# Four PSUM banks for logits and two for transposes, in place of two and four, in the first attention stage

## What is computed

```
_, sel = lax.top_k(score, k_top)
kv_sel = jax.vmap(lambda ck, ix: ck[ix])(c_kv, sel)
logits = jnp.einsum('bqhr,bqkr->bhqk', qa, kv_sel).astype(jnp.float32)
logits = logits + jnp.moveaxis(bias, -1, 1)
logits = jnp.where(valid[:, None], logits, -jnp.inf)
p = jax.nn.softmax(logits, axis=-1).astype(kv_sel.dtype)
return jnp.einsum('bhqk,bqkr->bqhr', p, kv_sel)
```

## Time and profile before

| what | value |
| --- | --- |
| median of 3 runs | 4300.61 us (4289.83 to 4303.97) |
| profiled execution, its own time | 4292.6 us |
| span of that execution | 4290.8 us |
| PE matmul busy | 3502.0 us (82%) |
| DVE busy | 2117.6 us (49%) |
| ACT busy | 2040.5 us (48%) |
| granted clock of PE, mean over the span | 0.906 |
| first attention stage (a_att) | 1238 to 2156 us of the span |
| second attention stage (b_att) | 3195 to 3997 us of the span |

### The profile page before, as it was taken

The page is one execution under the profiler, slowest core; times in us unless marked ns, Lnnn a source line. Parts: engine busy times, 40 slices in busy tenths (PEclk is TensorE's granted clock), DMA queues, the critical chain, the costliest instruction groups (busy, mean ns, idle before and its releaser), DMA issues. The chain is left out here.

```text
span 4290.8 us, 64366 instructions
## 1 busy us (share of the span) xinstructions
PE 3502.0 (82%) x18498; PEld 2627.5 (61%) x18498; DVE 2117.6 (49%) x5809; ACT 2040.5 (48%) x3499; POOL 524.7 (12%) x560
## 2 busy tenths in 40 slices
PE   5598577764049999999969499999988888899699
PEld 5487455653036666666658478888975555555587
DVE  0401288999955555555556500000017777777344
ACT  0412267988447777777722401111126666666322
POOL 0011000551001111111101011111100000000011
PEclk9898898865569999999989799999999999999789
DMA  5222533872012222222245222222221111110343
GB/s 121 99 67 65 173 70 123 227 211 80 27 52 82 77 77 76 76 74 75 65 165 176 98 76 71 73 71 71 69 76 46 43 43 47 43 48 29 120 132 113
DMA packets 361723, 378.40 MB, mean 88 GB/s; under 512 B 71792, under 2 KB 291344, under 8 KB 359952
## 3 DMA queue, kind: packets, MB, share of 16 engines
q1 hardware_dynamic: 361488, 375.35, 29.5%
HBM read 237.89 MB, written 137.36 MB: 87 GB/s over the span
## 5 line engine op out<-in xcount | busy, mean ns | idle before, releaser
L1002 DVE CUSTOM_DVE_ANT_0 a_att_sb_lg<-a_att_ps_s,mask 128x512 f32<-128x512 f32 (+3 forms) x512 | 302.7, 595 | 283.3 <-PE a_att_ps_s L896 240.3
L895 PE MATMUL a_att_ps_s<-a_att_sb_k,a_att_sb_q 128*128 128x512 f32 (+3 forms) x640 | 291.3, 455 | 169.9 <-DMA a_att_sb_k<-scratch_kT 153.5
L1076 ACT ACTIVATE a_att_sb_pT<-a_att_ps_t 128x512 f32<-128x512 f32 (+3 forms) x640 | 317.0, 530 | 146.6 <-PE a_att_ps_t L912 138.7
L494 ACT ACTIVATE b_qkgv_sb_o_lo<-b_qkgv_ps_acc 128x512 f32<-128x512 f32 x128 | 76.6, 598 | 637.7 <-PE b_qkgv_ps_acc L477 472.6
L912 PE MATMUL a_att_ps_t<-ident,a_att_sb_lg 128*128 128x128 f32 x2176 | 345.5, 282 | 38.6 <-issue 29.4
L1068 ACT ACTIVATE b_att_sb_lg<-b_att_sb_lg,b_att_sb_negm 128x384 f32<-128x384 f32 (+15 forms) x256 | 305.7, 1199 | 110.9 <-DVE b_att_sb_negm L1010 110.1
L1004 DVE TENSOR_SCALAR_CACHE_REDUCE b_att_sb_lg<-b_att_ps_s 128x512 f32<-128x512 f32 (+3 forms) x512 | 289.7, 591 | 137.4 <-PE b_att_ps_s L901 131.4
L1033 DVE MEMSET b_att_sb_mx<- 128x256 f32 x1 | 0.3, 272 | 721.8 <-PEq L88 721.8
L1068 ACT ACTIVATE a_att_sb_lg<-a_att_sb_lg,a_att_sb_negm 128x384 f32<-128x384 f32 (+15 forms) x256 | 307.4, 1201 | 81.6 <-DVE a_att_sb_negm L1010 81.6
L912 PEld LDWEIGHTS a_att_ps_t<-ident,a_att_sb_lg 128*128 128x128 f32 x2176 | 252.0, 142 | 148.7 <-issue 100.4
L901 PE MATMUL b_att_ps_s<-b_att_sb_k,b_att_sb_q 64*128 64x512 f32 (+3 forms) x1280 | 323.2, 592 | 14.0 <-DMA b_att_sb_k<-scratch_kT 9.9
(11 more groups left out here) (273 smaller groups left out, 7135.1 us busy)
## 6 DMA issues: line engine op xcount, KB each, us to landing
select_sb_mod_w<-in_mod_w SPq DMA_DIRECT2D x16, 1024.0 KB, 7.1
a_att_sb_q<-scratch_qT SPq DMA_DIRECT2D x128, 128.0 KB
a_att_sb_q<-scratch_qT SPq DMA_DIRECT2D x256, 64.0 KB
a_att_sb_k<-scratch_kT SPq DMA_DIRECT2D x64, 256.0 KB
b_qkgv_sb_w<-in_b_w_in SPq DMA_DIRECT2D x32, 512.0 KB
mod_sb_w<-in_mod_w SPq DMA_DIRECT2D x4, 2048.0 KB, 8.7
scratch_gateT<-a_gate_sb_o_lo SPq DMA_DIRECT2D x32, 256.0 KB, 2.4
scratch_qT<-select_sb_o_hi SPq DMA_DIRECT2D x32, 256.0 KB, 3.4
```

The costliest lines, as they stand in the source:

```text
L895: nc.tensor.matmul(out, q[:, p // 2 % QS, 0, cols], k[:, slot, a:z], start=True, stop=False)
L1002: x = nc.vector.tensor_tensor_reduce(out, src, tab, 1.0, 2 * NEG, ALU.add, ALU.max, top[:, col:col + 1])
L1076: nc.scalar.activation(pT[:, r % 2, a:z, c:c + P], t_ps[:, n % TR, 0:z - a], ACT.Copy).then_inc(t_left, 1)
```

## The change

In `stage_attention`, the ring of logits in PSUM has four chunks and the ring of transposes two quads, for both callers. For `b_att` these were the numbers before, so only `a_att` changes.

```
     V2 = M == 1
     width = HD if V2 else P
-    SR, TR = (2, 4) if V2 else (4, 2)
+    SR, TR = 4, 2
     NCHUNK = M * BEFORE[NB]
```

## The result

| | before | changed |
| --- | --- | --- |
| median | 4298.69 us (20 runs, 4289.0 to 4309.37) | 4312.85 us (20 runs, 4303.7 to 4320.28) |
| ratio to before | | 1.0031, interval 1.0023 to 1.004 |
| span of the profiled execution | 4290.8 us | 4318.2 us |
| first attention stage in it | 918 us | 930.5 us |

What follows compares the result with a forecast made beforehand. PE was taken as the bound of `a_att`. 1.1 + 1.3 - 0.2 = 2.2 us a head, 35 us in 16 heads, gave 4328 on the profiled execution or 4336 on the median, written as 4332; range 4301 to 4370.

Steps and rivals of the forecast that it cites:

- What bounds the kernel: In `a_att`, PE bounds: head 7 busy 55.8 of 57 us; its stops wait for DVE or would wait for ACT's copies.
- the rival on the clock: Stops of 1 us cost PE its clock in two places of each head: 4 to 5 us a head more, 4400; chance 0.03.
- Part 1: Two more logits banks: all 48.8 us of PE's waits for DVE go; no wait for the fourth chunk back.
- Part 2, place 4: Two transpose banks fewer, head 7: T(3,0) starts at 51.02 instead of 51.01, so zero late; savings of earlier chunks are lost.
- Part 2, places 5 and 6: T(4,2) waits for the copy of T(4,0), 0.3 us late; the saved 0.9 us are gone.
- Part 2, places 7 to 9: Chain through maximum, exponential and copy: T(5,2) 0.6 us late, T(6,2) 1.3, T(7,2) 1.1.
- The ring stops: Places 10 to 13: four waits for a transpose bank, 1.3 us together, against two DVE waits of 0.1 us that go.
- The sum: All heads of `a_att`: 1.1 + 1.3 - 0.2 = 2.2 us a head, 35 us in 16 heads.
- heads of 59 to 60 us: Sign expected in the profile after the change: `a_att` heads take 59 to 60 us; 57 us or shorter would refute the forecast.
- the two cancel: Rival: gain and loss cancel within 0.3%, 13 us, at the lower bound or a little less; chance 0.10.
- The bound below: Places 5 to 9 hold PE up nowhere, 1.3 us ring stops stay, 0.9 us returns: +0.4 us a head, 6 us.
- ACT as the bound of the large places: Rival: ACT's copies are pulled apart and exponentials queue at places 5 to 9: +64 us, 4365; chance 0.12.

## Why the prediction was right in sign and wrong in size

- *What bounds the kernel* held: PE, and its two sorts of stop. DVE as the releaser is gone, ACT has come, in eight places of a head, the longest 1.1 us, as foretold; the 4.1 us a head are just above the 2.5 to 4. The mean clock of the stage stayed at 0.97 and that of head 7 at 1.00, so the rival on the clock can go.
- *Part 1* held: no wait for the fourth chunk back.
- *Part 2, place 4*: T(3,0) 0.05 us late, forecast zero, but by luck. The prediction read that T(3,0) before already ended on the copy of T(2,0). With four transpose banks it does not wait for that copy, and its row has no idle time in front; it came right behind S(5,0), which had waited 0.31 us for DVE. With two banks it does wait. ACT in the changed kernel:

```profile
1662.28 0.19 ACT L1068 ACTIVATION_READ_ACCUMULATOR a_att_sb_lg<-a_att_sb_lg,a_att_sb_negm  x1
1662.37 0.96 ACT L1076 ACTIVATE a_att_sb_pT<-a_att_ps_t 128x512 f32<-128x512 f32 x2
```

  The profile puts T(3,0)'s stop of 0.97 us down to the exponential, but that had ended 0.59 us before T(3,0) began (1663.06). The copy of T(2,0), about 0.6 us from 1662.37, had ended 0.09 before. The 0.05 us for a release, read from that coincidence, held all the same: T(5,2) began at 1674.00, the copy of T(5,0) at 1673.35, and such a copy takes 0.60. The stop at T(3,0) is there in nine heads, 8.7 us together, where the waits put down to the exponential rose by 8.4.
- *Part 2, places 5 and 6* is the step that failed. It said that the maximum of place 5 would get "only about 0.1 us earlier", because DVE has two chunks to do first, and that T(4,2) would be 0.3 late. DVE's timeline at place 5, before and then changed (the one piece of S(5,1) with the read of its maximum, the first piece of S(5,2), and after rows left out the maximum of the place):

```profile
1653.24 0.69 DVE L1002 CUSTOM_DVE_ANT_0 a_att_sb_lg<-a_att_ps_s,mask 128x512 f32<-128x512 f32 x1
1653.86 0.08 DVE L1002 DVE_READ_ACCUMULATOR2_ANT a_att_sb_mx<- 128x1 f32 x1
1654.30 0.42 DVE L1002 CUSTOM_DVE_ANT_0 a_att_sb_lg<-a_att_ps_s,mask 128x256 f32<-128x256 f32 x1 [0.36 <-PE a_att_ps_s L896]
...
1655.21 0.16 DVE L1010 TENSOR_REDUCE a_att_sb_negm<-a_att_sb_mx 128x1 f32<-128x8 f32 x1
```

```profile
1665.10 0.69 DVE L1002 CUSTOM_DVE_ANT_0 a_att_sb_lg<-a_att_ps_s,mask 128x512 f32<-128x512 f32 x1
1665.71 0.08 DVE L1002 DVE_READ_ACCUMULATOR2_ANT a_att_sb_mx<- 128x1 f32 x1
1665.71 0.42 DVE L1002 CUSTOM_DVE_ANT_0 a_att_sb_lg<-a_att_ps_s,mask 128x256 f32<-128x256 f32 x1
...
1666.62 0.16 DVE L1010 TENSOR_REDUCE a_att_sb_negm<-a_att_sb_mx 128x1 f32<-128x8 f32 x1
```

  Before, DVE itself stood 0.36 us waiting for S(5,2), because PE had been waiting for DVE. Without it the maximum comes at 1666.62, where 1655.21 plus 12.00 would be 1667.21: 0.59 us sooner, not 0.1. S(5,1) itself starts 0.14 sooner, about what the walk allowed; the rest is the pause of 0.36 and the read of 0.08, which now lies under the next row. So T(4,2) is 0.2 early in place of 0.3 late, and this 0.5 us is in every later line of the table. The run with two and two banks shows that this is what the walk left out. There PE still waits for DVE, and T(4,2), T(5,2), T(6,2) and T(7,2) of head 7 are 0.40, 0.67, 1.16 and 0.88 us late, close to the forecast's 0.3, 0.6, 1.3 and 1.1. The walk told what two banks fewer for transposes cost and gave nothing for the maxima that two more banks for logits bring forward.
- *Part 2, places 7 to 9*: the chain was right, the spacing behind a stop was not. T(5,2) to S(7,3) was put at 0.56 us, as in the earlier trace rows; after a stop it is 0.39 (1674.00 to 1674.39). The forecast is 0.54 us too late at T(5,2), 0.75 at T(6,2), 0.84 at T(7,2) and 1.1 at T(8,0). Some 0.2 of this growth is the spacing behind T(5,2), and 0.26 that behind T(7,2) and T(7,3) (0.39 and 0.43 us to the next chunk's load where it was 0.55 and 0.53).
- *The ring stops* were sized nearly right: 1.3 less 0.2, so 1.1 us a head forecast, 1.03 measured between T(8,0) and the next head. That they are the loss is shown by the run with later quads in places 10 to 13, and that the other banks do not touch them by the run with two and two.
- *The sum* took 16 equal heads. From the first chunk of the first head to that of the last, 15 heads, the changed kernel takes 12.0 us more. Nine of these heads have no long stop and lose 9.3 us; six have one and lose 2.7, from 1.9 us more to 0.6 less. Behind T(8,0) those six lose the same 1.03 us; they differ before it, around the long stop, where T(3,0) comes 0.9 to 2.8 us sooner than before. Why was not tried. The sign "heads of 59 to 60 us" was meant for the mean of all heads (57.4 before): 58.2 was measured. T(6,2) was 0.55 late, just past the 0.5 that the prediction had set for being wrong.
- *The rivals*: the truth lies between the forecast and the second, "the two cancel": they cancel in places 4 to 9 and not in 10 to 13. The bound below, +6 us, was made of this very case, but it counted 0.9 us a head back that did not come. The low end of the range, 4301, is not that bound rounded up: 4292.6 and 6 are 4299. ACT as the bound of the large places did not show: in the run with all quads later a place takes 4.42 us with the same exponential and copies.
- The rule of the Trainium skill that was weighed (Perfetto Trace Analysis, Optimization Strategies) gave -48.8 us. The waits that it means did go, and the kernel became slower. With the order on PE changed as well it is 34 us faster, so the gain that the rule looks for came only once the new wait was taken away too.

## What to carry to other kernels

Banks of PSUM moved from one ring to another move a wait; read both rings, and for the one that shrinks ask what long instruction its consumer has in front of the copies. If a producer's stream is in a fixed order, it is worth ordering it so that the work with free banks stands where the consumer is busy: here the order and the banks each lost alone, 50 and 14 us, and won 34 together. When a wait between two engines goes, both get earlier, so neither's old start times can be kept in the walk through the chain.

## What was not expected of the hardware

After a stop the next loads of PE follow more closely: four transposes and then a chunk's load stand 0.39 us apart when the four began after a wait of 1.00 us, and 0.56 us when PE came to them without one. It is 0.39 as well behind the stop of 0.28 us at T(7,2) (1683.58 to 1683.97), so it does not grow with the stop. So 0.17 us of a stop on the rows of loads was no loss. And rows of DVE with a running maximum begin before the row ahead has ended: a piece of 512 columns lasts 0.69 us and the next starts 0.61 us behind its start (1665.10 to 1665.71), one of 256 columns lasts 0.42 us and the next starts 0.35 behind. Their durations overlap and must not be added.
